# Ending the output projection's first step tile by tile, gating inside PSUM, and moving three groups of copies and sums

## The chip, the cores and the metric

The kernel runs on one core of one Trainium2 chip. The metric is the time of one execution in microseconds (us), as the device measures it; the median of three runs is compared. Beside the timed runs one execution was taken by the hardware profiler, and all rows below come from it. A core has a matrix engine (TensorE, PE in the rows; PEld is its weight load), VectorE (DVE), ScalarE (ACT), GpSimd (POOL) and SyncE (SP), which here only issues DMA transfers. Matrix products land in PSUM, eight banks of 128 x 512 fp32 (the tensor `ps`, indexed by bank); everything else lies in SBUF.

## What is computed

One layer of a diffusion backbone over 1024 tokens of width 1024 (cut to what matters here):

```
y_x = merge(fourier_branch, retention_branch)        # (1024, 1024)
x   = x + g1 * (y_x @ w_out)                         # the "output projection" and its gated residual
h2  = rms_norm(x) * norm2_gain * (1 + sc2) + sh2
x   = x + g2 * (square(relu(h2 @ w_mlp1)) @ w_mlp2)  # MLP, D_FF = 4096
out = rms_norm(x) * final_gain
```

## The kernel before, in words

**Three products for one.** Each fp32 operand is split into a rounded part (`_hi`, made by ACT) and a remainder (`_lo`, made by DVE or POOL), and a product is three matmuls: hi x hi, hi x lo, lo x hi (`mm3`, lines 2159 to 2161). There is no scheduler: each engine has its own instruction list, written out by hand, and waits on semaphores. An engine runs its list strictly in order.

**The output projection** has 16 output tiles (128 tokens x 512 channels), in 4 steps of 4 tiles. Steps 0 and 1 are the two column halves of tokens 0 to 511, steps 2 and 3 those of tokens 512 to 1023. A tile sums over 8 channel tiles `kt`, in 4 weight chunks `kp` of two each (`("wo", n)` in a ring of six slots; ACT rounds a chunk at line 852, POOL makes its remainder at line 772). Step 0 is written apart (`out_first`): for each `kp` it first does the two matmuls with `yT_hi` for all four tiles (lines 2546, 2547: 16 matmuls), and then the one with `yT_lo` for all four (line 2553: 8 matmuls), since the last rows of `yT_lo` come late (line 1790 on DVE, the eighth channel tile). Steps 1 to 3 (`out_step`) use `mm3` and do a chunk's six matmuls of one tile behind each other. Tile i goes to bank `out_bank(i)` and may start when `o_free` is at least i - 3.

**The gated residual** (`residual(step, t)` on DVE) takes a finished tile out: it multiplies the bank by the gate row `g1b` into the SBUF tile `gated` (line 1801) and then adds `gated` to the x rows in `acc` (line 1804). `o_free` counts the multiplications, `x2_done` the additions of a token tile's second half; the stores to `x2_scr` on SP and the squares on ACT (`z_square`) wait for `x2_done`.

**The up projection** (`up(p, j)` on PE, lines 2632 to 2645) works by seven products p = 1 to 7 for each column pair j = 0 to 15, combined with sums of operands and results. A `up` is 12 matmuls. From j = 1 on the order on PE is (1, j+1), (3, j), (2, j+1), (4, j), (6, j+1), (5, j+1), (7, j+1). Products 1, 6, 7 and 4 pile up in one bank; between two of them ACT copies the bank out (`copy_up`, line 1238, into `uw` or `uv`), and the next waits for that copy. DVE adds such a copy to another bank (`add_up`, line 1981) when a quadrant of the result is complete; (3, j) may start when the sum "22" of its pair has been made. Weights of pair j + 2 are loaded, summed (`w_sums`, lines 1891 to 1897), rounded (`w_his`, line 1186) and split (`w_los`, line 1903) meanwhile, unit by unit, in the order of `LATER_UNITS` = B11, B21, T2, T1, T3, B22, T4. `ff_sums` (lines 1993 to 2000) sums results for the down projection.

**The down projection** (`down(s)` on PE, s = 0 to 111) has seven passes q = 0 to 6 of 16 steps n, each of 12 matmuls. Six slots (`LEAD`) hold the operands of coming steps; per step DVE makes two remainders (`s_lo` line 2043, `t_lo` line 2047) and in most passes one sum (line 2035 in pass 2, `b<-t_raw,b`), and PE's step waits for them. Between these, DVE takes finished results out: in passes 2 and 5, `take` (line 2084) and `add_gated` (lines 2079, 2080) add one block of 128 x 512 to the stream `x2`, one block behind each of the steps n = 5, 6, 7 and 8:

```
if q == 2 and 5 <= n < 9:
    dve.wait_ge(down_copied, n - 4)
    take(1, n - 5, BANK_C, p1)
    add_gated(n - 5, 0, (n - 5) % 2)
```

## Time and profile before

| what | us |
|---|---|
| median of 3 runs (lowest, highest) | 1341.75 (1339.44, 1341.82) |
| the profiled execution's own time | 1339.81 |
| its span, first to last instruction | 1338.0 |
| PE busy in the span | 1303.7 |
| DVE / ACT / POOL busy | 806.1 / 559.9 / 185.9 |

The mean granted TensorE clock of the span is 0.996 of full speed (2.4 GHz). A row's "busy" counts an instruction from start to end; matmuls are pipelined, so that the next one starts before the last has ended.

### The profile page before, as it was taken

To read this page: it belongs to the slowest core of one execution; us is meant where nothing else is said; L and a number is where in the kernel's file an instruction comes from. 1 tells how busy PE (TensorE), PEld (TensorE's weight loads), DVE (VectorE), ACT (ScalarE), POOL (GpSimd) and SP (SyncE) were. 2 spreads that over 40 slices of the span, in tenths; PEclk is the share of its full clock that TensorE was granted. 3 is DMA by queue.
4 is the path that set the end of the run, shared out by engine and by line. 5 is a ranking of instruction groups with operands and counts; after the bars stand their busy time and mean duration, and the time that the engine had idled before them with its cause. 6 is when DMAs were issued, how large, how long until landed. Compare 5 with 4: busy or idle time off the path is not lost.

```text
span 1338.0 us, 16538 instructions
## 1 busy us (share of the span) xinstructions
PE 1303.7 (97%) x6236; PEld 1063.6 (79%) x6236; DVE 806.1 (60%) x1270; ACT 559.9 (42%) x939; POOL 185.9 (14%) x103
## 2 busy tenths in 40 slices
PE   4999999999999999999999999999999999999997
PEld 0878788888888788888788878888888887888886
DVE  3563577752663434347568765665564678768866
ACT  5872221241121112114367754555454543545444
POOL 1116330111332222212450000000000000000000
PEclk9899999999999999999999999999999999999999
DMA  9304220201254444438533354444437987568634
GB/s 377 146 32 142 80 95 1 64 28 49 66 176 136 126 127 139 128 112 313 171 128 118 126 173 155 153 163 137 153 124 253 318 278 236 164 190 272 193 105 163
DMA packets 88471, 204.35 MB, mean 153 GB/s; under 512 B 11700, under 2 KB 11956, under 8 KB 87368
## 3 DMA queue, kind: packets, MB, share of 16 engines
q1 hardware_dynamic: 75552, 170.18, 38.0%
q10 hardware_dynamic: 11048, 26.82, 6.3%
q0 software_dynamic: 1792, 6.29, 1.4%
q8 instruction: 50, 0.82, 0.3%
q14 instruction: 29, 0.24, 0.1%
HBM read 159.72 MB, written 43.53 MB: 152 GB/s over the span
## 4 chain that ended last, share of the span: by engine, by line
PE 90%; DVE 4%; DMA 4%; ACT 1%; issue 1%; SPq 1%; ACTq 0%; DVEq 0%
PE ps L2159 19%; PE ps L2161 19%; PE ps L2160 19%; PE ps L2632 7%; PE ps L2640 7%; PE ps L2635 7%; PE ps L2658 3%; DMA raw<-in_w_stream 2%; PE ps L2230 2%; PE ps L2351 1%; PE ps L2197 1%; DMA ada_raw<-in_w_ada 1%; PE ps L2205 1%; PE ps L2333 1%; PE ps L2292 1%
## 5 line engine op out<-in xcount | busy, mean ns | idle before, releaser
L772 POOL TENSOR_TENSOR ring_lo<-raw,ring_hi 128x1024 fp32r<-128x1024 f32 x58 | 140.7, 2433 | 484.0 <-ACT ring_hi L852 483.9
L2159 PE MATMUL ps<-t_hi,s_hi 128*128 128x512 f32 x392 | 153.2, 391 | 1.2 <-DVE t_lo L2047 1.2
L2161 PE MATMUL ps<-t_hi,s_lo 128*128 128x512 f32 x392 | 153.1, 391 | 0.0
L2160 PE MATMUL ps<-t_lo,s_hi 128*128 128x512 f32 x392 | 153.1, 391 | 0.0
L2159 PE MATMUL ps<-hT_hi,ring_hi 128*128 128x512 f32 x320 | 125.0, 391 | 0.0
L2161 PE MATMUL ps<-hT_hi,ring_lo 128*128 128x512 f32 x320 | 124.5, 389 | 0.0
L2160 PE MATMUL ps<-hT_lo,ring_hi 128*128 128x512 f32 x320 | 124.5, 389 | 0.0
L1268 ACT ACTIVATE s_hi<-s_raw 128x512 fp32r<-128x512 f32 x112 | 70.6, 630 | 117.1 <-DMA b<-in_w_stream 57.5
L852 ACT ACTIVATE ring_hi<-raw 128x1024 fp32r<-128x1024 f32 x62 | 64.9, 1057 | 110.7 <-PE ps L2161 53.8
L2043 DVE TENSOR_TENSOR s_lo<-s_raw,s_hi 128x512 fp32r<-128x512 f32 x112 | 77.3, 690 | 47.9 <-ACT s_hi L1268 47.4
L1754 DVE SCALAR_TENSOR_TENSOR ada_acc<-ada_raw,silu_c,ada_acc 128x1024 f32<-128x1024 f32 x28 | 44.4, 1584 | 98.6 <-DMA ada_raw<-in_w_ada 98.4
L2159 PE MATMUL ps<-ring_hi,hT_hi 128*128 128x512 f32 x232 | 94.1, 406 | 0.0
L2161 PE MATMUL ps<-ring_hi,hT_lo 128*128 128x512 f32 x232 | 90.6, 391 | 0.0
L2160 PE MATMUL ps<-ring_lo,hT_hi 128*128 128x512 f32 x232 | 90.5, 390 | 0.0
L2159 PEld LDWEIGHTS ps<-t_hi,s_hi 128*128 128x128 f32 x392 | 73.6, 188 | 17.6 <-DVE t_lo L2047 1.8
L2161 PEld LDWEIGHTS ps<-t_hi,s_lo 128*128 128x128 f32 x392 | 73.6, 188 | 15.8
L2160 PEld LDWEIGHTS ps<-t_lo,s_hi 128*128 128x128 f32 x392 | 73.6, 188 | 15.8
L2159 PEld LDWEIGHTS ps<-hT_hi,ring_hi 128*128 128x128 f32 x320 | 60.1, 188 | 14.9 <-issue 2.6
L2161 PEld LDWEIGHTS ps<-hT_hi,ring_lo 128*128 128x128 f32 x320 | 60.1, 188 | 12.6
L2160 PEld LDWEIGHTS ps<-hT_lo,ring_hi 128*128 128x128 f32 x320 | 60.1, 188 | 12.3
L1256 ACT ACTIVATE ffa<-ffa 128x512 f32<-128x512 f32 x48 | 30.3, 631 | 73.6 <-DVE ffa L1981 73.6
L2159 PEld LDWEIGHTS ps<-ring_hi,hT_hi 128*128 128x128 f32 x232 | 43.6, 188 | 10.6 <-issue 1.5
(404 smaller groups left out, 2807.9 us busy)
## 6 DMA issues: line engine op xcount, KB each, us to landing
s_raw<-ff_scr SPq DMA_DIRECT2D x112, 256.0 KB, 2.9
raw<-in_w_stream SPq DMA_DIRECT2D x50, 512.0 KB, 3.6
ada_raw<-in_w_ada ACTq DMA_DIRECT2D x32, 512.0 KB, 4.3
ff_scr<-ffs SPq DMA_DIRECT2D x16, 1024.0 KB, 5.1
t_raw<-in_w_stream SPq DMA_DIRECT2D x64, 256.0 KB, 3.4
w_B_raw<-in_w_stream SPq DMA_DIRECT2D x48, 256.0 KB, 2.8
ff_scr<-ffa SPq DMA_DIRECT2D x16, 768.0 KB, 4.5
b<-in_w_stream SPq DMA_DIRECT2D x48, 256.0 KB, 4.5
```

The source lines that it names most:

```text
L772: nc.gpsimd.tensor_tensor(lo_ap, raw_of(i), hi_ap.bitcast(F32), ALU.subtract).then_inc(split, 1)
L852: A(slot(c)[0], raw_of(i), ACT.Copy).then_inc(hi_done, 1)
L1268: A(s_slot[n][0][:], s_slot[n][2][:], ACT.Copy).then_inc(down_hi, 1)
L1754: do.chain(V.scalar_tensor_tensor(ada_acc[:], ada_raw[:], silu_c[:, kt, 0:1], ada_acc[:], ALU.mult, ALU.add), ada_acc_done)
L2043: V.tensor_tensor(s_slot[n][1][:], s_slot[n][2][:], s_slot[n][0][:].bitcast(F32), ALU.subtract).then_inc(down_lo, 1)
L2159: M(dst, lhsT=l_hi, rhs=r_hi, start=first, stop=False, skip_group_check=goes_on)
L2160: M(dst, lhsT=l_hi, rhs=r_lo, start=False, stop=False, skip_group_check=goes_on)
L2161: return M(dst, lhsT=l_lo, rhs=r_hi, start=False, stop=last, skip_group_check=goes_on)
L2632: M(ps[:, b, :], lhsT=l_hi[:, w], rhs=m_hi[:, kt, :], start=kt == 0 and not adds, stop=False, skip_group_check=adds)
L2635: M(ps[:, b, :], lhsT=l_hi[:, w], rhs=m_lo[:, kt, :], start=False, stop=False, skip_group_check=adds)
L2640: mm = M(ps[:, b, :], lhsT=l_lo[:, w], rhs=m_hi[:, kt, :], start=False, stop=kt == 3 and (p, j) != (6, 0), skip_group_check=adds)
L2658: mm = M(ps[:, down_bank(q, sub), :], lhsT=left[:, sub * P:(sub + 1) * P], rhs=right[:], start=False, stop=False)
```

## The change

It has four parts.

1. Step 0 of the output projection keeps `out_first` for `kp` = 0 to 2; its last chunk (`kp` = 3, channel tiles 6 and 7) is done by a new function `out_first_end`, tile by tile: six matmuls for a tile, then the next tile. The matmuls are the same 24, in another order.
2. `residual` writes the gated product back to its PSUM bank and adds from there; `gated` goes. `o_free` now counts the additions, and takes over what `x2_done` did (`row_added`).
3. In the up projection the pair behind j = 2 is ordered like that behind j = 1: ACT's `copy_up(6, 3)` stands ahead of the rounding of T2 and T1, `copy_up(7, 3)` ahead of T3, B22 and T4, and DVE's sum "22" of pair 3 ahead of the remainders of T3, B22 and T4.
4. In passes 2 and 5 of the down projection the four blocks for `x2` stand behind steps n = 5, 7, 9 and 11.

```
@@ -281,7 +281,6 @@
         hq = place("hq", o_t, [P, KT, 2 * P])
         g1b = place("g1b", o_t + 8192, [P, D])
         b1b = place("b1b", o_t + 14336, [P, D])
-        gated = place("gated", o_t + 12288, [P, 512])
 
         junk3 = place("junk3", o_t + 8192, [P, D])
 
@@ -392,7 +391,6 @@
         g_ready = sem("g_ready")
         o_done = sem("o_done")
         o_free = sem("o_free")
-        x2_done = sem("x2_done")
         a_hi = sem("a_hi")
         a11_lo = sem("a11_lo")
         a12_lo = sem("a12_lo")
@@ -532,6 +530,10 @@
 
             return i - 2 if i in (2, 3) else 4 + i % 4
 
+        def row_added(eng, t):
+
+            eng.wait_ge(o_free, t + (5 if t < 4 else 9))
+
         def main_wait(eng, i):
 
             if i >= 2:
@@ -589,7 +591,7 @@
         @block.sync
         def _(sp):
             def store_x2(t):
-                sp.wait_ge(x2_done, t + 1)
+                row_added(sp, t)
                 sp.dma_start(x2_scr[t], acc[:, t % 4, :]).then_inc(x2_stored[t % 4], 16)
 
             sp.dma_start(dist[:], ins["dist"]).then_inc(decay_in, 16)
@@ -1113,7 +1115,7 @@
             hi_to(("wo", 12))
 
             def z_square(t):
-                act.wait_ge(x2_done, t + 1)
+                row_added(act, t)
                 act.wait_ge(sumsq, 10 + t)
                 if t == 0:
                     act.wait_ge(gates_done, 2 * KT)
@@ -1317,18 +1319,20 @@
                     w_his(j + 2, LATER_UNITS[:2])
                 if j > 1:
                     relu_square("21", j)
+                if j == 2:
+                    copy_up(6, j + 1)
                 if j + 2 < FP:
                     w_his(j + 2, LATER_UNITS[2:4])
-                if j == 1:
+                if j in (1, 2):
                     copy_up(7, j + 1)
-                if j > 1 and not last:
+                if j > 2 and not last:
                     copy_up(6, j + 1)
                 if j == FP - 2:
                     down_his(0)
                 if j + 2 < FP:
                     w_his(j + 2, LATER_UNITS[4:])
                 if not last:
-                    if j > 1:
+                    if j > 2:
                         copy_up(7, j + 1)
                     relu_square("22", j + 1)
 
@@ -1798,10 +1802,10 @@
                 if nh == 0:
                     dve.wait_ge(acc_in[t % 4], 16 * (t // 4 + 1))
                 dve.wait_ge(o_done, i + 1)
-                do.chain(V.tensor_tensor(gated[:], ps[:, out_bank(i), :], g1b[:, nh * 512:(nh + 1) * 512], ALU.mult),
-                         o_free)
+                gated = ps[:, out_bank(i), :]
+                do.chain(V.tensor_tensor(gated, gated, g1b[:, nh * 512:(nh + 1) * 512], ALU.mult))
                 dst = acc[:, t % 4, nh * 512:(nh + 1) * 512]
-                do.chain(V.tensor_tensor(dst, dst, gated[:], ALU.add), x2_done if nh else None)
+                do.chain(V.tensor_tensor(dst, gated, dst, ALU.add), o_free, i + 1)
 
             def z_mean(first, last):
                 n = max(first - 3, 0) + 1
@@ -2065,11 +2069,14 @@
                 if j == 1:
                     add_up("22", j + 1)
                 ff_sums(j)
+                if j == 2:
+                    w_los(j + 2, LATER_UNITS[2:4])
+                    add_up("22", j + 1)
                 if j + 2 < FP:
-                    w_los(j + 2, LATER_UNITS[2:])
+                    w_los(j + 2, LATER_UNITS[4 if j == 2 else 2:])
                 if j == FP - 2:
                     down_los(0)
-                if j > 1 and not last:
+                if j > 2 and not last:
                     add_up("22", j + 1)
 
             def add_gated(t, nh, first, signal=None):
@@ -2116,10 +2123,11 @@
                     dve.wait_ge(x2_in, 16 * 2)
                 if s == 5 * FP + 4:
                     dve.wait_ge(x2_in, 16 * 4)
-                if q == 2 and 5 <= n < 9:
-                    dve.wait_ge(down_copied, n - 4)
-                    take(1, n - 5, BANK_C, p1)
-                    add_gated(n - 5, 0, (n - 5) % 2)
+                if q == 2 and n in (5, 7, 9, 11):
+                    t = (n - 5) // 2
+                    dve.wait_ge(down_copied, t + 1)
+                    take(1, t, BANK_C, p1)
+                    add_gated(t, 0, t % 2)
                 if q == 3 and 6 <= n < 10:
                     t = n - 6
                     dve.wait_ge(down_copied, 4 + t + 1)
@@ -2127,10 +2135,11 @@
                     do.chain(V.tensor_tensor(x2[:, t, 512:], x2[:, t, 512:], out_u[:, t % 2, :], ALU.add), x2_sum)
                 if q == 3 and 10 <= n < 14:
                     early_gain(n - 10)
-                if q == 5 and 5 <= n < 9:
-                    dve.wait_ge(down_copied, 8 + n - 4)
-                    take(4, n - 5, BANK_B, pw)
-                    add_gated(4 + n - 5, 1, (n - 5) % 2)
+                if q == 5 and n in (5, 7, 9, 11):
+                    t = (n - 5) // 2
+                    dve.wait_ge(down_copied, 8 + t + 1)
+                    take(4, t, BANK_B, pw)
+                    add_gated(4 + t, 1, t % 2)
                 if q == 5 and 9 <= n < 13:
                     early_gain(4 + n - 9)
                 if q == 5 and n == 14:
@@ -2540,7 +2549,7 @@
                     for e in range(2):
                         kt = 2 * kp + e
                         if t == 0:
-                            pe.wait_ge(*((y_hi_done, kt + 1) if kt < KT - 1 else (y_split, KT)))
+                            pe.wait_ge(y_hi_done, kt + 1)
                         cs = slice(e * 512, (e + 1) * 512)
                         toks = slice(t * P, (t + 1) * P)
                         M(ps[:, out_bank(t), :], lhsT=yT_hi[:, kt, toks], rhs=r_hi[:, cs], start=kt == 0, stop=False)
@@ -2549,19 +2558,30 @@
                     for e in range(2):
                         kt = 2 * kp + e
                         if t == 0:
+                            pe.wait_ge(y_split, kt + 1)
+                        mm = M(ps[:, out_bank(t), :], lhsT=yT_lo[:, kt, t * P:(t + 1) * P],
+                               rhs=r_hi[:, e * 512:(e + 1) * 512], start=False, stop=False)
+                mm.then_inc(used, 1)
+
+            def out_first_end():
+
+                r_hi, r_lo = chunk(("wo", 3))
+                for t in range(4):
+                    toks = slice(t * P, (t + 1) * P)
+                    for kt in (KT - 2, KT - 1):
+                        if t == 0:
                             pe.wait_ge(y_split, kt + 1 + (kt == KT - 1))
-                        mm = M(ps[:, out_bank(t), :], lhsT=yT_lo[:, kt, t * P:(t + 1) * P],
-                               rhs=r_hi[:, e * 512:(e + 1) * 512], start=False, stop=kt == KT - 1)
-                    if kp == 3:
-                        mm.then_inc(o_done, 1)
-                    elif t == 3:
-                        mm.then_inc(used, 1)
-
-            for kp in range(4):
+                        cs = slice(kt % 2 * 512, (kt % 2 + 1) * 512)
+                        mm = mm3(ps[:, out_bank(t), :], yT_hi[:, kt, toks], yT_lo[:, kt, toks], r_hi[:, cs], r_lo[:, cs],
+                                 False, kt == KT - 1)
+                    mm.then_inc(o_done, 1)
+
+            for kp in range(3):
                 out_first(kp)
                 if kp == 1:
                     pe.wait_ge(gates_done, 2 * KT)
                     reduce_row(3, 2)
+            out_first_end()
             for step in range(1, 3):
                 for kp in range(4):
                     for t in range(4):
```

How the first part moves instructions on PE, at the last chunk of step 0. Before, the last rows of the chunk: pairs of matmuls with the rounded `yT_hi` (two for each channel tile of a token tile), and then all eight with `yT_lo`, ahead of step 1, which begins with line 2159.

```order
L2546 MATMUL ps<-ring_hi,yT_hi 128x512
L2547 MATMUL ps<-ring_lo,yT_hi 128x512
L2546 MATMUL ps<-ring_hi,yT_hi 128x512
L2547 MATMUL ps<-ring_lo,yT_hi 128x512
L2553 MATMUL ps<-ring_hi,yT_lo 128x512 x8
L2159 MATMUL ps<-ring_hi,yT_hi 128x512
```

Now, from the end of the third chunk on (line 2562 is its eight matmuls with `yT_lo`); lines 2168 to 2170 are `mm3`, and two such threes are one tile.

```order
L2556 MATMUL ps<-ring_lo,yT_hi 128x512
L2562 MATMUL ps<-ring_hi,yT_lo 128x512 x8
L2168 MATMUL ps<-ring_hi,yT_hi 128x512
L2169 MATMUL ps<-ring_lo,yT_hi 128x512
L2170 MATMUL ps<-ring_hi,yT_lo 128x512
L2168 MATMUL ps<-ring_hi,yT_hi 128x512
L2169 MATMUL ps<-ring_lo,yT_hi 128x512
L2170 MATMUL ps<-ring_hi,yT_lo 128x512
```

The matmuls with `yT_lo` have moved from the end of the chunk to each tile's place, so a tile is complete after every sixth matmul of the chunk.

How the third part moves ACT's instructions, after the sum "12" and "11" of its turn j = 2. Line 1238 (1240 now) is `copy_up`, with `uv` for product 6 and `uw` for product 7; line 1186 (1188 now) rounds a unit of the weights. Before:

```order
L1250 ACTIVATE a_229<-ps 128x512
L1252 ACTIVATE a_229<-a_229 128x512
L1186 ACTIVATE w_T_hi<-w_T_raw 128x512 x2
L1238 ACTIVATE uv_231<-ps 128x512
L1186 ACTIVATE w_T_hi<-w_T_raw 128x512
L1186 ACTIVATE w_B_hi<-w_B_raw 128x512
L1186 ACTIVATE w_T_hi<-w_T_raw 128x512
L1238 ACTIVATE uw<-ps 128x512
```

Now:

```order
L1252 ACTIVATE a_228<-ps 128x512
L1254 ACTIVATE a_228<-a_228 128x512
L1240 ACTIVATE uv_230<-ps 128x512
L1188 ACTIVATE w_T_hi<-w_T_raw 128x512 x2
L1240 ACTIVATE uw<-ps 128x512
L1188 ACTIVATE w_T_hi<-w_T_raw 128x512
L1188 ACTIVATE w_B_hi<-w_B_raw 128x512
L1188 ACTIVATE w_T_hi<-w_T_raw 128x512
```

Both copies have moved up by one group of roundings.

And on DVE, in the same turn, from `ff_sums` on (line 1903, now 1907, makes a remainder; line 1981, now 1985, is `add_up`). Before:

```order
L2000 TENSOR_TENSOR ffs_227<-ffa_225,ffs_227 128x512
L1903 TENSOR_TENSOR w_T_lo<-w_T_raw,w_T_hi 128x512 x3
L1903 TENSOR_TENSOR w_B_lo<-w_B_raw,w_B_hi 128x512
L1903 TENSOR_TENSOR w_T_lo<-w_T_raw,w_T_hi 128x512
L1981 TENSOR_TENSOR ffa_226<-ps,uw 128x512
```

Now:

```order
L2004 TENSOR_TENSOR ffs_226<-ffa_224,ffs_226 128x512
L1907 TENSOR_TENSOR w_T_lo<-w_T_raw,w_T_hi 128x512 x2
L1985 TENSOR_TENSOR ffa_225<-ps,uw 128x512
L1907 TENSOR_TENSOR w_T_lo<-w_T_raw,w_T_hi 128x512
L1907 TENSOR_TENSOR w_B_lo<-w_B_raw,w_B_hi 128x512
L1907 TENSOR_TENSOR w_T_lo<-w_T_raw,w_T_hi 128x512
```

The sum stood behind five remainders and stands behind two.

## Rows read from the trace of the kernel before

**Rows 1.** The page's first part: engine, busy us (share of the span), instructions.

```profile
PE 1303.7 (97%) x6236; PEld 1063.6 (79%) x6236; DVE 806.1 (60%) x1270; ACT 559.9 (42%) x939; POOL 185.9 (14%) x103
```

**Rows 2.** PE's waits: line, releaser: us in total, times, longest.

```profile
PE ps L2256 <- DMA ada_in<-in_w_ada: 14.4, 8, 8.8
PE ps L2197 <- issue: 4.7, 1, 4.7
PE ps L2159 <- DVE gated L1801: 2.2, 2, 1.6
PE ps L2159 <- DVE t_lo L2047: 1.2, 1, 1.2
PE ps L2632 <- ACT uv L1238: 1.1, 1, 1.1
...
PE ps L2632 <- DVE ffa L1981: 0.7, 1, 0.7
```

**Rows 3.** Timeline of PE, projection: start, us, instruction, [idle before it <- releaser].

```profile
632.33 0.39 PE L2546 MATMUL ps<-ring_hi,yT_hi 128*128 128x512 f32 x1
...
635.96 1.98 PE L2553 MATMUL ps<-ring_hi,yT_lo 128*128 128x512 f32 x8
...
639.93 0.47 PE L2159 MATMUL ps<-ring_hi,yT_hi 128*128 128x512 f32 x1 [0.64 <-DVE gated L1801]
...
644.61 0.47 PE L2159 MATMUL ps<-ring_hi,yT_hi 128*128 128x512 f32 x1 [1.61 <-DVE gated L1801]
```

**Rows 4.** Timeline of DVE around the same place.

```profile
629.66 1.23 DVE L1790 TENSOR_TENSOR yT_lo<-y,yT_hi 128x1024 fp32r<-128x1024 f32 x1
...
636.71 0.69 DVE L1801 TENSOR_TENSOR gated<-ps,g1b 128x512 f32<-128x512 f32 x1 [4.56 <-PE ps L2553]
637.43 1.62 DVE L1804 TENSOR_TENSOR acc<-acc,gated 128x512 f32<-128x512 f32 x1
...
641.27 2.48 DVE L1804 TENSOR_TENSOR acc<-acc,gated 128x512 f32<-128x512 f32 x1
643.78 0.69 DVE L1801 TENSOR_TENSOR gated<-ps,g1b 128x512 f32<-128x512 f32 x1
```

**Rows 5.** Timeline of POOL there.

```profile
633.75 4.76 POOL L772 TENSOR_TENSOR ring_lo<-raw,ring_hi 128x1024 fp32r<-128x1024 f32 x2 [4.67 <-ACT ring_hi L852]
640.80 2.40 POOL L772 TENSOR_TENSOR ring_lo<-raw,ring_hi 128x1024 fp32r<-128x1024 f32 x1 [2.29 <-ACT ring_hi L852]
```

**Rows 6.** Line 1504 (rotary step): count: ns min/median/max, first and last start.

```profile
L1504 DVE TENSOR_TENSOR ps<-ps,rope x16: 699/700/700, 58.0 to 240.4; 128x512 f32<-128x512 f32 x16
```

**Rows 7.** Tile `acc`, the last of its four loads: issue and landing.

```profile
L1097 ACTq DMA_DIRECT2D acc<-in_x x1: 484/484/484, 623.0 to 623.0; - x1
...
DMA to landing us min/median/max: 8.7/8.7/8.7
```

**Rows 8.** Timeline of PE, up projection: first matmuls of (7, 3) and (3, 3).

```profile
783.57 0.47 PE L2632 MATMUL ps<-h_hi,w_T_hi 128*128 128x512 f32 x1 [1.09 <-ACT uv L1238]
...
789.98 0.47 PE L2632 MATMUL ps<-s_hi,w_B_hi 128*128 128x512 f32 x1 [0.72 <-DVE ffa L1981]
```

**Rows 9.** Timeline of ACT there.

```profile
782.85 0.58 ACT L1238 ACTIVATE uv<-ps 128x512 f32<-128x512 f32 x1
```

**Rows 10.** Timeline of DVE there.

```profile
779.74 0.69 DVE L1891 TENSOR_TENSOR w_T_raw<-w_B_raw,w_T_raw 128x512 f32<-128x512 f32 x1 [4.75 <-DMA w_B_raw<-in_w_stream]
...
786.14 1.89 DVE L1903 TENSOR_TENSOR w_T_lo<-w_T_raw,w_T_hi 128x512 fp32r<-128x512 f32 x3
...
789.15 0.68 DVE L1981 TENSOR_TENSOR ffa<-ps,uw 128x512 f32<-128x512 f32 x1
```

**Rows 11.** Timeline of DVE, pass 2 of the down projection: starts of steps 5, 9, 10.

```profile
1116.81 0.69 DVE L2035 TENSOR_TENSOR b<-t_raw,b 128x512 f32<-128x512 f32 x1
...
1133.49 0.69 DVE L2035 TENSOR_TENSOR b<-t_raw,b 128x512 f32<-128x512 f32 x1
...
1135.49 0.68 DVE L2035 TENSOR_TENSOR b<-t_raw,b 128x512 f32<-128x512 f32 x1
```

**Rows 12.** Timeline of PE, first matmul of step 9 of that pass.

```profile
1135.63 0.50 PE L2159 MATMUL ps<-t_hi,s_hi 128*128 128x512 f32 x1 [1.15 <-DVE t_lo L2047]
```

More of the change, by code:

```diff
@@ L283, in program @@
         b1b = place("b1b", o_t + 14336, [P, D])
-        gated = place("gated", o_t + 12288, [P, 512])
         junk3 = place("junk3", o_t + 8192, [P, D])
@@ L533, in out_bank, with row_added @@
             return i - 2 if i in (2, 3) else 4 + i % 4
+        def row_added(eng, t):
+            eng.wait_ge(o_free, t + (5 if t < 4 else 9))
         def main_wait(eng, i):
@@ L1319, in _ @@
                     relu_square("21", j)
+                if j == 2:
+                    copy_up(6, j + 1)
                 if j + 2 < FP:
                     w_his(j + 2, LATER_UNITS[2:4])
-                if j == 1:
+                if j in (1, 2):
                     copy_up(7, j + 1)
-                if j > 1 and not last:
+                if j > 2 and not last:
                     copy_up(6, j + 1)
@@ L2067, in _ @@
                 ff_sums(j)
+                if j == 2:
+                    w_los(j + 2, LATER_UNITS[2:4])
+                    add_up("22", j + 1)
                 if j + 2 < FP:
-                    w_los(j + 2, LATER_UNITS[2:])
+                    w_los(j + 2, LATER_UNITS[4 if j == 2 else 2:])
                 if j == FP - 2:
                     down_los(0)
-                if j > 1 and not last:
+                if j > 2 and not last:
                     add_up("22", j + 1)
@@ L2118, in _ @@
                     dve.wait_ge(x2_in, 16 * 4)
-                if q == 2 and 5 <= n < 9:
-                    dve.wait_ge(down_copied, n - 4)
-                    take(1, n - 5, BANK_C, p1)
-                    add_gated(n - 5, 0, (n - 5) % 2)
+                if q == 2 and n in (5, 7, 9, 11):
+                    t = (n - 5) // 2
+                    dve.wait_ge(down_copied, t + 1)
+                    take(1, t, BANK_C, p1)
+                    add_gated(t, 0, t % 2)
                 if q == 3 and 6 <= n < 10:
@@ L2129, in _ @@
                     early_gain(n - 10)
-                if q == 5 and 5 <= n < 9:
-                    dve.wait_ge(down_copied, 8 + n - 4)
-                    take(4, n - 5, BANK_B, pw)
-                    add_gated(4 + n - 5, 1, (n - 5) % 2)
+                if q == 5 and n in (5, 7, 9, 11):
+                    t = (n - 5) // 2
+                    dve.wait_ge(down_copied, 8 + t + 1)
+                    take(4, t, BANK_B, pw)
+                    add_gated(4 + t, 1, t % 2)
                 if q == 5 and 9 <= n < 13:
```

38 lines of the change are left out of this document (23 added, 15 removed).

## The prediction, made before the changed kernel had run

> **What bounds the kernel now.** I read the page's table of engines first: PE is busy for 1303.7 of 1338.0 us [rows 1], so no other engine's work can shorten the kernel, only PE's own waits can. Then PE's waits [rows 2]. The two longest stand in the start-up (lines 2256 and 2197), which the change does not touch. Behind the start-up five waits matter, together 5.2 us: two on `gated` (2.2), one on `t_lo` (1.2), one on `uv` (1.1), one on `ffa` (0.7). The change touches the making of all four. Then the timeline at each.
>
> A wait costs more than its idle time. Eight matmuls take 1.98 us and one 0.39 [rows 3], so they start (1.98 - 0.39) / 7 = 0.227 us apart; after a wait the engine idles from the end of the last one, which adds 0.39 - 0.23 = 0.16, and the first matmul lasts 0.47 or 0.50 instead of 0.39, which delays the next by 0.08 or 0.11. So each wait costs its idle time plus 0.24 (0.27).
>
> **Part 1 and 2, the projection.** Before: 0.64 + 0.24 and 1.61 + 0.24 = **2.73 us** [rows 3]. The reason is in [rows 4]: all four tiles of step 0 end within the last eight matmuls, DVE gets the first at 636.71, and then needs 0.72 for a multiplication (636.71 to 637.43) and 0.7 for an addition, if undisturbed. But the additions at 637.43 and 641.27 last 1.62 and 2.48, and end 0.54 and 0.55 us after POOL's instructions beside them (633.75 + 4.76 = 638.51; 640.80 + 2.40 = 643.20) [rows 5]. The multiplication at 636.71, with one input in PSUM, lasts 0.69 inside POOL's span.
>
> After, tile by tile. The chunk starts at 632.33; the last matmul of tile k (0 to 3) starts (6k + 5) x 0.227 later: 633.47, 634.83, 636.19, 637.55. DVE began 0.52 after such a start before (the first tile's second matmul with `yT_lo` started at 635.96 + 0.23 = 636.19, DVE at 636.71). So the tiles are there at 633.98, 635.35, 636.71 and 638.07. A residual is a multiplication from PSUM into PSUM, for which line 1504 shows the form, 0.70 us [rows 6], and an addition with one input in PSUM, taken as 0.69 like the multiplication of the kernel before; with the hand-overs of 0.03 seen there 1.45 in all. The additions end at 635.43, 636.88, 638.33 and 639.78. PE restarted 0.14 after the releasing instruction (643.78 + 0.69, 644.61), and would want the four banks at 637.78 + 0.227 x 6k: 637.78, 639.14, 640.50, 641.86. The spare time is 2.2, 2.1, 2.0 and 1.9 us: both waits go, and the later release (behind the addition, +0.73) costs nothing while this cover stands. Without it, each bank would come 0.73 later.
>
> What could spoil it. The eighth channel tile's remainder is now wanted at the fourth matmul, 632.33 + 3 x 0.227 = 633.01, where it was wanted at 636.19; it ends at 629.66 + 1.23 = 630.89 [rows 4]: 2.1 spare. The x rows: the last load was issued at 623.0 and landed 8.7 later, 631.7 [rows 7], ahead of 633.98. Bounds for what has no row of its own (an addition out of PSUM right behind a write into it): from 0.69 up to 1.2, as if half again were added; at 1.2 a residual takes 1.96 and the fourth ends at 633.98 + 7.84 = 641.82, 0.1 us late for PE. **Gain 2.73, at least 2.6.**
>
> The Trainium skill ("SBUF — State Buffer", section "Who interferes with whom") says that a VectorE instruction with two SBUF inputs contends with a GpSimd instruction that reads SBUF, and that one with at most one SBUF input does not. Both halves agree with the rows above. By it the new additions are never caught; without it, see the second rival.
>
> **Part 3, the up projection.** Before: 1.09 + 0.24 and 0.72 + 0.24 = **2.29 us** [rows 8]. The first: (7, 3) waits for ACT's copy into `uv` at 782.85 [rows 9], which stands behind two roundings, and these behind DVE's weight sums, which begin at 779.74 when a load has landed after 4.75 us of idling [rows 10]. Now the copy stands ahead of them. It needs only (6, 3), which ends 12 matmuls (2.72 us) ahead of (5, 3)'s end, so it is done long before (7, 3) comes up. That wait goes: (7, 3) starts at 783.57 - 1.09 - 0.16 = 782.32. (1, 4) follows, and (3, 3) comes up 24 matmuls later, at 787.77.
>
> The second: (3, 3) waits for the sum "22", at 789.15 [rows 10], and restarted at 789.98, 0.83 after its start. DVE's queue up to there is still tied to the load at 779.74; three remainders in a row take 1.89, so one frees the queue after 0.60 ((1.89 - 0.69) / 2). The sum now stands behind two remainders: 786.14 + 1.20 = 787.34. Its other input, `uw`, needs (7, 3) done (782.32 + 11 x 0.227 + 0.39 = 785.2) and one copy of 0.6: 785.9, earlier. So (3, 3) starts at 787.34 + 0.83 = 788.17: a wait of 0.40 stays, with 0.08 behind it. **Gain 2.29 - 0.48 = 1.81.** Bounds: 1.33, if the second wait stays whole, and 2.29. Behind the moved copies ACT's three other roundings and DVE's three remainders are about 1 us later; they serve products of pair 4 that PE reaches over 10 us later, since a turn of seven products takes 19 us.
>
> **Part 4, the down projection.** Before: 1.15 + 0.27 = **1.42 us** [rows 12]. Step 5 of pass 2 begins on DVE at 1116.81 and step 9 at 1133.49: 4.17 us a step with a block for `x2`, 2.00 without (to 1135.49) [rows 11], against 2.72 on PE. So DVE falls back by 1.45 a step four times over, and the remainder of step 9 ends just ahead of PE's restart at 1135.63, that is 2.08 after the step's start. PE wanted it 1.31 earlier, at 1134.32.
> With the blocks at 5, 7, 9 and 11 step 12 starts at 1116.81 + 4 x 4.17 + 3 x 2.00 = 1139.49 and its remainder ends at 1141.57; PE wants it at 1134.32 + 3 x 2.72 = 1142.48. That is the narrowest place: 0.9 spare (step 10: 1.6). The wait goes. DVE is never waiting for loads there, so its own pace decides. **Gain 1.42**, bounds 0.5 (if 0.9 more than the spare time is lost) and 1.42. Pass 5 has no wait of PE [rows 2], and its blocks come later but long before pass 6 needs their bank.
>
> **The sum.** 2.73 + 1.81 + 1.42 = 5.96 us. Everything behind the projection is set off by PE or by loads that PE's progress releases, so the time should reach the end. The profiled execution took 1339.81 (span 1338.0): 1333.85 and 1332.0. That execution lies 1.9 below the median of 1341.75, near the fastest of the three (1339.44); set against the median the forecast is 1341.75 - 6.0 = **1335.7**. The smallest difference that can be told from none is about 0.2%, 2.7 us.
>
> **The rivals.**
> 1. *One wait comes back.* DVE at step 12 has 0.9 to spare and the sum "22" is tied to a load. If the down wait returns and the second up wait stays whole, 5.96 - 1.42 - 0.48 = 4.1 is left: 1337.7. For it: both chains hang on DVE's pace. Against it: both are worked out from one trace in which they fit. Still faster than the bound.
> 2. *The additions are caught by POOL although one input is in PSUM.* Then the addition at 634.71 ends at 639.05 as that of 637.43 did, tile 1's at 640.50, and tile 2's at 643.75 like the one at 641.27. PE is held at 640.64 (1.5 late) and at 643.89, 3.4 late in all, and up to 2.2 more if a third is caught. Against 2.73 before that is a loss of 0.7 to 2.9; with the other gains (3.23) the kernel takes 1339.2 to 1341.4. Against it: the multiplication at 636.71.
> 3. *The time does not reach the end*, because a load or a later wait grows by as much (say at the load that ended 4.75 us of idling on DVE): around 1341, no difference. Against it: between the named places PE shows no wait of note, and the loads are released by PE.
> 4. *The other side: the release behind the addition.* A bank is now held for both operations, four in a row 5.8 us. If the first residual starts at T, the fourth bank is there for PE at T + 5.94, against 644.61 before. With T = 633.98 this is hidden; from T = 638.7, 4.7 us later, this stage is slower than before, and to end 2.7 us slower in all T must lie at 644.6 (3.23 more for the other gains). What can shift T is the last remainder: it stands behind two instructions that POOL holds back, and one more such delay is at most a POOL instruction, 2.4 us; that would cost PE 0.3. It would take several: 1344.5 or more.
>
> **How the numbers follow.** All three stages as worked out: 0.73. Rival 1: 0.15. Rival 2: 0.04. Rival 3: 0.05. Rival 4: 0.03. The terms' bounds give gains of 2.6 + 1.33 + 0.5 = 4.4 to 6.44, so 1335.3 to 1337.3; the median of three lies anywhere in a spread of 2.4 us (1339.44 to 1341.82), mostly downwards from the middle. Range 1333.2 to 1338.2, which takes in rival 1. Faster: 0.73 + 0.15 = 0.88; same: rivals 2 and 3, 0.09; slower: 0.03.
>
> **What would show it.** PE's waits: no entry for the residual's lines or for `uv`; `t_lo` gone; at the sum "22" a wait of about 0.2 idle. The residual's additions all at 0.7, also inside POOL's spans. DVE's first residual at 634.0. Wrong would be: additions of 1.6 to 2.5 us, a wait at 633 for line 1794's `yT_lo`, or a `t_lo` wait at step 12.

## The result, and the profile after

| | before | after |
|---|---|---|
| median us (lowest to highest), 5 runs each, side by side | 1339.44 (1338.0 to 1341.82) | 1332.25 (1330.96 to 1332.83) |
| span of the profiled execution | 1338.0 | 1330.4 |

The ratio is 0.9947, 95% interval 0.9935 to 0.9959: faster by 7.2 us, with 5.5 to 8.7 by the interval. The five runs of before include the three whose median was 1341.75. The direction and all three places are as forecast. The time is 3.4 us below the 1335.7 forecast and 0.95 below the range.

PE's busy time has not changed (1304.2 against 1303.7 in [rows 1]); what has gone is waiting. The waits of PE after (line, releaser: us in total, times, longest), to be held against [rows 2]:

```profile
PE ps L2265 <- DMA ada_in<-in_w_ada: 13.6, 7, 8.5
PE ps L2206 <- issue: 2.7, 1, 2.7
PE ps L2239 <- ACT kT L859: 1.0, 4, 0.3
PE ps L2273 <- DVE mod_rows L1482: 0.8, 1, 0.8
PE ps L2239 <- ACT xh_b L1136: 0.2, 1, 0.2
```

No entry is left for the residual, `uv`, `ffa` or `t_lo`; only the start-up and small waits on transposes remain. The timeline of DVE in the projection (start, us, instruction, idle before it), against [rows 4]; lines 1806 and 1808 are the multiplication and the addition:

```profile
628.50 1.22 DVE L1794 TENSOR_TENSOR yT_lo<-y,yT_hi 128x1024 fp32r<-128x1024 f32 x1
...
632.83 0.70 DVE L1806 TENSOR_TENSOR ps<-ps,g1b 128x512 f32<-128x512 f32 x1 [1.85 <-PE ps L2170]
633.56 0.69 DVE L1808 TENSOR_TENSOR acc<-ps,acc 128x512 f32<-128x512 f32 x1
634.28 0.70 DVE L1806 TENSOR_TENSOR ps<-ps,g1b 128x512 f32<-128x512 f32 x1
...
637.93 0.69 DVE L1808 TENSOR_TENSOR acc<-ps,acc 128x512 f32<-128x512 f32 x1
```

and that of POOL and PE beside it:

```profile
632.89 4.87 POOL L774 TENSOR_TENSOR ring_lo<-raw,ring_hi 128x1024 fp32r<-128x1024 f32 x2 [4.97 <-ACT ring_hi L854]
```

```profile
631.17 0.39 PE L2168 MATMUL ps<-ring_hi,yT_hi 128*128 128x512 f32 x1
...
636.61 0.39 PE L2168 MATMUL ps<-ring_hi,yT_hi 128*128 128x512 f32 x1
```

The last chunk begins 1.16 earlier in this execution than in the trace of before (631.17, 632.33 in [rows 3]), so the first residual was due at 633.98 - 1.16 = 632.82, and began at 632.83. The additions last 0.69 inside POOL's span, where additions with two inputs in SBUF lasted 1.62 and 2.48 [rows 4]; a residual takes 1.45 (634.28 - 632.83). Step 1 follows the 24 matmuls without a gap (636.61 - 631.17 = 24 x 0.227).

The up projection, DVE (against [rows 10]) and PE:

```profile
781.96 1.29 DVE L1907 TENSOR_TENSOR w_T_lo<-w_T_raw,w_T_hi 128x512 fp32r<-128x512 f32 x2
783.16 0.68 DVE L1985 TENSOR_TENSOR ffa<-ps,uw 128x512 f32<-128x512 f32 x1
```

```profile
783.99 0.47 PE L2652 MATMUL ps<-s_hi,w_B_hi 128*128 128x512 f32 x1
```

The sum "22" stands 1.20 behind the start of the remainders, as forecast, and (3, 3) starts 0.83 behind it. Its start comes 0.51 after that of the matmul before, so a delay of 0.28 is left, with 0.08 behind it (0.40 and 0.08 forecast). In the down projection's pass 2 the steps with a block take 4.17 and those without 2.00, as forecast, and PE does not wait at step 12, which begins on DVE at the last of these rows:

```profile
1111.46 0.69 DVE L2039 TENSOR_TENSOR b<-t_raw,b 128x512 f32<-128x512 f32 x1
1115.62 0.69 DVE L2039 TENSOR_TENSOR b<-t_raw,b 128x512 f32<-128x512 f32 x1
1117.62 0.69 DVE L2039 TENSOR_TENSOR b<-t_raw,b 128x512 f32<-128x512 f32 x1
...
1134.12 0.69 DVE L2039 TENSOR_TENSOR b<-t_raw,b 128x512 f32<-128x512 f32 x1
```

The remainder that PE needs for this step was ready barely in time: in down_only, where PE did wait for it, PE restarted 2.14 behind the start of DVE's step 12 (1139.63 to 1141.77), which here gives 1134.12 + 2.14 = 1136.26, and PE begins its step 12 at

```profile
1136.38 0.40 PE L2168 MATMUL ps<-t_hi,s_hi 128*128 128x512 f32 x1
```

That leaves 0.12 us to spare in this execution, where 0.9 was forecast.

The mechanisms are there one for one. The question that the experiments had to answer is where the other 1.2 us of gain come from, and the 2.3 by which the median of the first three runs of before (1341.75) lay above that of all five (1339.44).

**How stretches are measured.** Between the first matmul of the projection with `yT_hi`, the first of the up projection and the first of the down projection PE's work is the same in every kernel here, so the distances between these matmuls in PE's timeline, and that to PE's last, show what each stage loses. In a trace of after they are 93.63, 303.23 and 312.30, in the trace of before 96.51, 305.16 and 313.88: 2.88 + 1.93 + 1.58 = 6.39 us. The 1.16 by which the projection began earlier stands ahead of them all and belongs to the start-up, which the change does not touch.

### The profile page after: what moved, and what is told of

Its sections match the earlier page's. It is cut to its first block, busy times and chain, and to the rows that moved or that the text cites. A ratio compares the mean times of both kernels' runs of the same rounds, so it can differ in the third digit from the quotient of the medians.

```text
span 1330.4 us, 16538 instructions
## 1 busy us (share of the span) xinstructions
PE 1304.2 (98%) x6236; PEld 1064.5 (80%) x6236; DVE 801.0 (60%) x1270; ACT 560.4 (42%) x939; POOL 185.9 (14%) x103
## 4 chain that ended last, share of the span: by engine, by line
PE 95%; DMA 2%; DVE 1%; ACT 1%; SPq 0%; issue 0%; ACTq 0%; DVEq 0%
PE ps L2168 20%; PE ps L2170 20%; PE ps L2169 20%; PE ps L2652 7%; PE ps L2660 7%; PE ps L2655 7%; PE ps L2678 3%; DMA raw<-in_w_stream 2%; PE ps L2239 2%; PE ps L2360 1%; PE ps L2206 1%; PE ps L2214 1%; PE ps L2342 1%; PE ps L2301 1%; PE ps L2208 1%; PE ps L2352 1%
```

## The experiments

The theory when they began: the terms are right in kind, and the size is off by what one execution shows. The rivals: another part of the kernel gains too; or the parts are worth something else than was argued. Ratios are to runs of the kernel before on the same chip, with 95% intervals; the columns "stretches" are the three above.

| kernel | median us | ratio | stretches |
|---|---|---|---|
| before_again | 1338.88 | 1.0001 (0.9992 to 1.001) | 97.38, 304.96, 314.46 |
| before_third | 1341.18 (one run) | | 97.79, 305.01, 314.27 |
| before_fourth | 1336.41 (one run) | | 95.16, 305.09, 314.13 |
| tile_end (part 1) | 1335.93 | 0.9973 (0.9962 to 0.9984) | 93.78, 305.01, 314.30 |
| psum_only (part 2) | 1336.79 | 0.998 (0.9971 to 0.9989) | 94.55, 305.14, 313.49 |
| tile_end_psum (1 and 2) | 1335.49 | 0.9971 (0.996 to 0.9981) | 93.63, 304.97, 314.59 |
| up_only (part 3) | 1337.57 | 0.9983 (0.9974 to 0.9992) | 97.36, 303.25, 315.00 |
| down_only (part 4) | 1337.6 | 0.9985 (0.9976 to 0.9994) | 97.03, 304.96, 312.73 |
| three_parts (without part 2) | 1331.66 | 0.9944 (0.993 to 0.9958) | 93.69, 303.27, 312.30 |
| after_again | 1331.48 | 0.9942 (0.9929 to 0.9954) | 93.63, 303.27, 312.30 |
| two_more | 1331.36 | 0.9938 (0.9925 to 0.995) | 93.63, 302.71, 312.30 |
| gates_early | 1336.83 | 0.9978 (0.9968 to 0.9989) | 97.31, 305.09, 312.30 |

**The kernel before, and the changed one, once more.** No edit.

> The kernel before, unchanged, profiled once more. Two theories on the 1.2 us by which the changed kernel's trace is ahead already at the first matmul on yT_hi (613.66 against 614.82 us), a place that the change does not touch. Chance of the start-up (loads of ada_in, the first weights): this trace lies anywhere between some 613 and 616 at that place, and before the first ring_hi,hc_hi matmul it waits for a time other than the 4.7 us seen. Layout of the program: it comes at 614.8 again. Both: ratio 1.000 within its interval; behind that place the trace repeats 96.5 us to the first up product, 305.2 to the first down step and 313.9 to PE's end, within 0.3.

> The changed kernel once more. If its gain is the sum of the three stages, 6.4 us, and the rest chance: ratio 0.9952, within 0.9942 to 0.9962, and the place of the first yT_hi matmul somewhere else than 613.66. If the 7.2 us seen are the change's own: 0.9947 again and that place at 613.7 again.

The expectation that before_again would repeat 96.5, 305.2 and 313.9 within 0.3 failed in two of three stretches (97.38 and 314.46). Stretches in which PE has no wait repeat within 0.01 us (93.63 in four traces, 312.30 in five; only three_parts has 93.69). The start of the projection, 614.82 in the trace of the prediction and 613.66 in that of after, came at 612.59 in before_again and 612.71 in after_again, and lies between 612.59 and 614.82 in all fourteen traces, so the 1.16 between the first two is chance of the start-up and not a difference of the programs. The ratio of after_again, 0.9942, lies on the edge of the 0.9942 to 0.9962 expected for a gain of 6.4 us. The waits of PE in before_again:

```profile
PE ps L2159 <- DVE gated L1801: 3.2, 2, 1.9
...
PE ps L2159 <- DVE t_lo L2047: 1.5, 2, 1.2
```

These were 2.2 and 1.2 in [rows 2], with one wait on `t_lo`, not two.

**Part 1 alone.** The last chunk tile by tile, `gated` in SBUF as before:

```
-            for kp in range(4):
+            for kp in range(3):
                 out_first(kp)
...
+            out_first_end()
```

> Only the new order of the last chunk of step 0; the gated product goes through SBUF and the bank is free behind the multiplication, as before. My theory (POOL holds back the additions with two SBUF inputs): the first residual starts 2.7 us earlier, but its addition waits for POOL's pair of instructions, and the third addition for the next one, so that PE waits about 0.8 and 2.0 us: nearly the 2.7 of before; ratio 1.000, change 0 to -0.6 us. Rival (the spacing of the tiles is what counts, POOL or not): both waits go, -2.7 us, ratio 0.998.

My theory fell, and the rival held: part 1 alone takes nearly the whole loss out of the stretch (93.78, where 93.63 is left without any wait). The timeline of DVE shows why:

```profile
632.77 0.69 DVE L1801 TENSOR_TENSOR gated<-ps,g1b 128x512 f32<-128x512 f32 x1 [1.99 <-PE ps L2161]
...
634.95 2.05 DVE L1804 TENSOR_TENSOR acc<-acc,gated 128x512 f32<-128x512 f32 x1
637.03 0.69 DVE L1801 TENSOR_TENSOR gated<-ps,g1b 128x512 f32<-128x512 f32 x1
637.76 2.05 DVE L1804 TENSOR_TENSOR acc<-acc,gated 128x512 f32<-128x512 f32 x1
639.85 0.69 DVE L1801 TENSOR_TENSOR gated<-ps,g1b 128x512 f32<-128x512 f32 x1
```

```profile
640.68 0.47 PE L2159 MATMUL ps<-ring_hi,yT_hi 128*128 128x512 f32 x1
```

Two additions are still held, and last 2.05 us. But DVE starts on the first tile 3.8 us ahead of PE's step 1 (636.55), where it was 1.1 in before (636.71, with the 24 matmuls from 632.33 over at 637.78), and here a bank is released by the multiplication. The last bank is free at 639.85 + 0.69 = 640.54, and PE, which wants it at 640.64 (24 + 18 matmuls after the chunk's start at 631.11), starts at 640.68: no idle time, but nothing to spare either.

**Part 2 alone, and with part 1.**

```
-                do.chain(V.tensor_tensor(gated[:], ps[:, out_bank(i), :], g1b[:, nh * 512:(nh + 1) * 512], ALU.mult),
-                         o_free)
+                gated = ps[:, out_bank(i), :]
+                do.chain(V.tensor_tensor(gated, gated, g1b[:, nh * 512:(nh + 1) * 512], ALU.mult))
...
-                do.chain(V.tensor_tensor(dst, dst, gated[:], ALU.add), x2_done if nh else None)
+                do.chain(V.tensor_tensor(dst, gated, dst, ALU.add), o_free, i + 1)
```

> Only the gated product in PSUM, with the release behind the addition; the order of the last chunk as before. My theory: additions all 0.7, releases at 1.45 us steps from the first tile at 636.7, so PE waits about 0.5 once and 0.1 three times: 0.8 in place of 2.8, change -2.0 us, ratio 0.9985. Rival (the later release costs): the bank comes 0.7 later each time, PE waits 2.7 or more, no gain.

> Both parts in the projection, nothing else. My theory: no wait of PE between the first projection matmul and the first up product; -2.8 us, ratio 0.9979; the stretch from the first yT_hi matmul to the first up product 93.6 us as in the whole change. If the whole change's 7.2 us were more than the sum of its parts, this would show less than -2.5.

Alone, part 2 makes all additions 0.69, and 0.92 us of loss is left (94.55 against 93.63, 0.8 expected), so the rival of a later release that costs the whole gain is out. It leaves one wait of PE, on the first addition, since the bank now comes behind both operations and the tiles still end together:

```profile
636.13 0.47 PE L2161 MATMUL ps<-ring_hi,yT_hi 128*128 128x512 f32 x1 [0.35 <-DVE acc L1806]
```

Together they give the 93.63 that was expected, without a wait of PE. The two parts do not add: 3.2 us and 2.4 us alone, 3.3 together, all against 96.93, the mean of the stretch over the seven traces in which both places are as before the change.

**The change without part 2.** As this says that part 2 is worth 0.15 at most, it was tried: the changed kernel with `residual`, `o_free` and `x2_done` as before.

> The changed kernel without its part 2 (the gated product is again put into an SBUF tile, and a bank is released behind the multiplication). My theory from the runs so far: once the tiles end six matmuls apart (part 1), the additions are still held until a POOL instruction ends (two of them at 2.05 us in the run of part 1 alone), but the spacing and the release behind the multiplication absorb it, so part 2 is worth only the 0.15 us by which the stretch from the first matmul of the projection to the first of the up projection was longer there (93.78 against 93.63). Expected: that stretch 93.7 to 93.9, PE without a wait on `gated` over 0.1 us, the time within 0.3 us of the changed kernel's, ratio to before 0.9945. The rival (the prediction's reading: both parts are needed, since DVE is held by POOL): a wait on `gated` of 1 us or more comes back, stretch 95 or more, ratio 0.9955 or higher.

The theory held: 93.69, no wait on `gated`, a ratio that can't be told from that of the whole change. Three additions are held and last 1.87, 2.05 and 2.30 us, and PE does not wait for them:

```profile
632.86 1.87 DVE L1806 TENSOR_TENSOR acc<-acc,gated 128x512 f32<-128x512 f32 x1
...
635.49 2.05 DVE L1806 TENSOR_TENSOR acc<-acc,gated 128x512 f32<-128x512 f32 x1
...
639.75 2.30 DVE L1806 TENSOR_TENSOR acc<-acc,gated 128x512 f32<-128x512 f32 x1
```

**Parts 3 and 4 alone.**

```
+                if j == 2:
+                    w_los(j + 2, LATER_UNITS[2:4])
+                    add_up("22", j + 1)
```

```
-                if q == 2 and 5 <= n < 9:
+                if q == 2 and n in (5, 7, 9, 11):
```

> Only the earlier copies and sum in the up projection. My theory: the wait for uv goes, of the wait for the sum 22 some 0.3 to 0.5 stays; the stretch from the first up product to the first down step falls from 305.2 to 303.3 us, change -1.9 us, ratio 0.9986. Rival (the gain needs the shift of the projection): the wait comes back with the load it hangs on, under 1 us.

> Only the blocks for x2 in every second step. My theory: the t_lo wait goes, the stretch from the first down step to PE's end falls from 313.9 to 312.3 us, change -1.5 us, ratio 0.9989, and step 12's remainder ends 0.9 us ahead of PE. Rival (DVE's total is what counts): the wait moves to a later step and the gain is under 0.7.

Part 3 takes the up stretch from 305.04 (mean of the nine traces with the old order) to 303.25: 1.8 us, in every trace alike. The gain does not need the shift of the projection, so the rival is out, and the wait that is left is 0.2, not 0.3 to 0.5. Part 4 brings the down stretch to 312.73, where 312.3 was expected: most of the gain, so DVE's total is not what counts, but one short wait is left, at step 12, in this execution:

```profile
1141.77 0.50 PE L2161 MATMUL ps<-t_hi,s_hi 128*128 128x512 f32 x1 [0.18 <-DVE t_lo L2047]
```

Step 5 began on DVE 101.40 after the first matmul of the down projection here, and 100.32 in the trace of the prediction (1116.81 - 1016.49), for which 0.9 to spare was worked out. A start 1.08 later should then have been about 0.2 too late. PE was in fact 0.34 late (0.18 of idle time and the 0.16 by which the idle time is shorter than the delay), so the trace of the prediction had 0.7 to spare and not 0.9. That place is indeed the narrowest.

**A step more in the same direction.** In the changed kernel the sum "22" of pair 3 stands ahead of all five remainders; and `residual(3, 7)` stands ahead of `s2_sum(0)`.

```
                 if j == 2:
-                    w_los(j + 2, LATER_UNITS[2:4])
                     add_up("22", j + 1)
...
-            s2_sum(0)
             residual(3, 7)
+            s2_sum(0)
```

> The changed kernel with the sum 22 of pair 3 ahead of all five remainders, and the last residual of the projection (3, 7) ahead of s2_sum(0). My theory: the wait of 0.28 + 0.08 at (3, 3) and the one of 0.41 at the transposes of xh behind the second up product both go: -0.8 us against the changed kernel, ratio to before 0.9946 if that has 0.9952. Rival: s2_sum, 1.45 later, holds back s1_sum and the weight sums of pair 1, and a wait appears at the first up products that takes it back.

The up stretch loses another 0.52 to 0.56 (0.8 expected), and `ffa` and `xh_b` are gone from the waits, with no new wait in their place, so the rival is out; in the total (1331.36 against 1331.48 in after_again) that can't be told from nothing.

**Two more executions of the kernel before.** No edit.

> The kernel before, unchanged, once more. Theory on the size of the miss: the waits that the change removes differ from one execution to the next, and the one trace of the prediction had short ones. Over the runs that kept the old order they cost 2.8 to 3.7 us in the projection and 1.1 to 2.7 us in pass 2 of the down projection. Expected here: projection 93.63 plus 2.8 to 3.7 = 96.4 to 97.4, from the first down projection matmul to PE's end 312.30 plus 1.1 to 2.7 = 313.4 to 315.0, and in pass 2 a cost that rises with the start of DVE's step 5 relative to PE's. Rival (the waits are steady, and the miss is a difference of executions outside these stretches): 96.5 and 313.9 again, each within 0.1.

> The same kernel a fourth time, with the same expectations: projection 96.4 to 97.4 and down projection 313.4 to 315.0 by the theory of waits that vary, 96.5 and 313.9 by the rival. The sum over both stretches, averaged over the traces of the kernel before, should come out 0.9 to 1.4 us above that of the trace of the prediction.

The down stretches lie within what was expected (314.27 and 314.13). The waits in the projection vary more than I said: 97.79 and 95.16, where 96.4 to 97.4 was expected, and so the mean over the four traces of the kernel before lies only 0.5 above the first one (sum of projection and down stretches: 410.39, 411.84, 412.06, 409.29), not 0.9 to 1.4. The rival of steady waits is out. What makes them vary: an addition that is held ends 0.55 after POOL's instruction, so its length is set by where in POOL's instruction it begins. In before_fourth, of the first four additions only the second and the fourth were caught, and one of the two waits was absent:

```profile
635.21 0.69 DVE L1804 TENSOR_TENSOR acc<-acc,gated 128x512 f32<-128x512 f32 x1
...
636.66 2.05 DVE L1804 TENSOR_TENSOR acc<-acc,gated 128x512 f32<-128x512 f32 x1
...
639.47 0.69 DVE L1804 TENSOR_TENSOR acc<-acc,gated 128x512 f32<-128x512 f32 x1
```

In before_third two were caught early in POOL's instructions and lasted 2.83 and 2.54 us, and the stretch is the longest.

**What sets the wait in the down projection.** Over the eight traces that keep the old order of both blocks and loads, what PE loses in pass 2 (the starts of its matmuls that come more than 0.227 apart) goes with the start of DVE's step 5, counted from the first matmul of the down projection:

| | psum_only | before | fourth | third | tile_end | again | tile_end_psum | up_only |
|---|---|---|---|---|---|---|---|---|
| step 5 starts | 99.90 | 100.32 | 100.58 | 100.68 | 100.76 | 100.87 | 101.05 | 101.45 |
| PE loses | 1.13 | 1.50 | 1.75 | 1.88 | 1.92 | 2.08 | 2.23 | 2.65 |

The difference is 98.77 to 98.84 everywhere. From step 2 to step 5 DVE does not wait (7.24 us), and step 2 waits for a load; in before:

```profile
1109.57 0.69 DVE L2035 TENSOR_TENSOR b<-t_raw,b 128x512 f32<-128x512 f32 x1 [4.26 <-DMA t_raw<-in_w_stream]
```

SP issues it right behind three loads that are wanted only at step 4:

```profile
1099.67 0.43 SPq L733 DMA_DIRECT2D g2b<-mod_scr  x1
1100.14 0.43 SPq L734 DMA_DIRECT2D b2b<-in_b_ada  x1
1100.62 0.43 SPq L735 DMA_DIRECT2D fgb<-in_final_gain  x1
...
1101.91 0.59 SPq L714 DMA_DIRECT2D t_raw<-in_w_stream  x1
```

So they were issued 23 steps earlier, in the kernel before, with nothing else changed:

```
-                if s == 2 * FP + 1:
+                if s == FP - 6:
                     sp.wait_ge(row_stored, 16 * 8)
                     sp.dma_start(g2b[:], mod_scr[3:4, :].to_broadcast([P, D])).then_inc(gates_in, 16)
```

> The kernel before, with the three broadcast loads of `g2b`, `b2b` and `fgb` issued 23 steps earlier (behind step 10 of pass 0, not behind step 1 of pass 2). In the traces so far the load of `t_raw` for step 2 of pass 2 stands right behind them in SP's queue and lands 7.6 us after its issue, where 3.7 is the median; DVE waits for it, and the cost in pass 2 is the start of step 5, counted from the first matmul of the down projection, less 98.81. Theory (these loads make step 2's load late, and so set the wait): step 2 starts on DVE at or before 91.5 instead of 92.6 to 94.2, step 5 at 98.8 or earlier, PE has no wait on `t_lo` in pass 2, and the stretch from the first matmul of the down projection to PE's end is 312.3 to 312.6, with the time at about 1337.3 by this alone. Rival (the load is late because all DMA engines are busy with the weights of pass 1, whatever stands ahead of it): step 2 still starts at 92.6 or later, with 1.1 to 2.7 us of waits and a stretch of 313.4 to 315.0.

The theory held. The load for step 2, issued 85.4 us after the first matmul of the down projection in both kernels, landed 3.0 us after its issue and not 7.6 (7.2 to 8.8 in the thirteen traces with the old order of loads). Step 2 starts at 88.48, step 5 at 97.04 (98.8 is where waiting begins), and PE has no wait on `t_lo`, with the blocks still at 5, 6, 7 and 8. The rows of DVE's steps 2 and 3:

```profile
1104.98 0.68 DVE L2035 TENSOR_TENSOR b<-t_raw,b 128x512 f32<-128x512 f32 x1
1107.64 0.69 DVE L2035 TENSOR_TENSOR b<-t_raw,b 128x512 f32<-128x512 f32 x1 [0.59 <-DMA t_raw<-in_w_stream]
```

The stretch is 312.30, as in the changed kernel, and the ratio 0.9978 (1.5 to 4.3 us) agrees with a loss of about 2 us. This edit together with part 4 was not run.

## Why the prediction was right, and where it was wrong

**The time that the gain was taken from: wrong, and the main error.** The step that failed is "set against the median the forecast is 1341.75 - 6.0 = 1335.7". The profiled execution had taken 1339.81, and 1341.75 was the middle of three runs, a small sample: sets of 5 to 25 runs of the same kernel give medians of 1338.59 to 1339.44. The same gain of 6.0 taken from the profiled execution gives 1333.85, and from 1339.44 it gives 1333.5, 1.2 us above the measured time. The text had both figures and chose the one that did not go with the terms: all terms were read from the execution of 1339.81. Of the 3.4 us by which the forecast missed, 2.3 lie here (1341.75 - 1339.44), and the rest in the size of the gain. It took both to leave the range of 1333.2 to 1338.2: with the gain right and only this time wrong the kernel would have taken 1339.44 - 5.96 = 1333.5, and with this time right and only the gain wrong 1341.75 - 7.2 = 1334.55.

**The size of the gain: 5.96 forecast, 7.2 measured, too small by 1.2.** 5.96 lies in the interval of the ratio, 5.5 to 8.7, but the traces show where the rest is. The means of the traces with the old order are 96.93 for the projection (seven traces), 305.04 for up (nine) and 314.27 for down (eight); less 93.63, 303.25 and 312.30:

| term | forecast | same pair of traces | mean of the traces |
|---|---|---|---|
| projection | 2.73 | 2.88 | 3.30 |
| up | 1.81 | 1.93 | 1.79 |
| down | 1.42 | 1.58 | 1.97 |
| sum | 5.96 | 6.39 | 7.06 |

The mis-sized terms are thus the first and the third: "0.64 + 0.24 and 1.61 + 0.24" and "1.15 + 0.27" were one execution's waits. Over the traces these waits cost between 1.5 and 4.2 us in the projection and between 1.1 and 2.7 in the down projection. Within the one pair of traces 0.43 more went than was added up: 0.12 because less of the second up wait stayed (0.36, not 0.48), the rest mostly in delays of under 0.1 us each on PE that the text did not count. The range took the spread of the medians into account and not that of the waits: its bound of 6.44 was the largest gain that the one trace allowed.

**Parts 1 and 2: the mechanisms right, their roles wrong.** The first residual started within 0.01 us of its forecast time, a residual took the 1.45 that was worked out, and no addition with an input in PSUM was held. That "both waits go" holds; but the prediction left open which part does it, and its "the reason is in [rows 4]" puts the held additions beside the tiles that end together. three_parts shows that the spacing alone is enough: the holds are there and cost nothing. Part 2 only gives the spare time back that the holds take: at the fourth bank tile_end has nothing left (it starts 0.04 late), where after has the 1.9 that was worked out (the fourth addition ends at 638.62, and 0.14 later is 638.76; PE wants the bank at 640.70). Rival 2's price (0.7 to 2.9 us worse) rested on holds together with the release behind the addition, a pair that no kernel here has.

**Part 3: right.** The first wait goes, of the second 0.28 + 0.08 is left (0.40 + 0.08), and no run brought it back.

**Part 4: right in kind, and narrower than said.** "0.9 spare" at step 12 was 0.7, as down_only shows, and 0.12 in the trace of after, whose step 5 started later (100.94 against 100.32). It is a reserve against the load of step 2, and step 5 started up to 1.13 later in other executions (101.45): the four traces with parts 1, 3 and 4 (after, after_again, three_parts and two_more, 100.27 to 100.94) show no wait, and down_only, at 101.40, does. That pass 2 lost nothing there is thus partly luck, and by the latest start seen, 101.45, the changed kernel could lose an estimated 0.5 us there in some executions. The prediction said that DVE "is never waiting for loads there, so its own pace decides". From step 2 on that is so; but where its pace begins is set by the load at step 2, with 4.26 us of idling just ahead of the rows that it had read, and the same load, delayed by three others, is why before waited there at all (gates_early).

**Rivals.** 1 happened in a small form once (down_only, 0.43 us). 2 did not: no addition with an input in PSUM was caught. 3 and 4 did not: what PE saved reached the end whole. From the end of PE's last matmul to that of the span it is 7.6 us in every trace.

## What to carry to other kernels

A wait read from one trace is one draw: where what ends it is a load's landing, or the place of one engine's instruction within another's, profile the same kernel two or three times and take the mean before pricing its removal, and take the gain from the time of the execution that the terms were read from. For a wait of an engine that runs at its own pace, follow the chain back to where it last stood still; taking three loads out of the way of the one that it had stood still for removed the wait as well as a change to the pace did. When tiles that are taken out by another engine all end together, try spacing their ends first: here that alone gave 3.2 us, and with it in place the shorter additions gave less than 0.2 more.

## What the runs showed of the hardware

**A slower clock that cost nothing.** In before_third PE stood still for 1.84 us, and half a microsecond later its matmuls started 0.39 and then, seven times, 0.43 apart instead of 0.227. PE's rows, and the same core in windows (the third number from the end, 0.50 and 1.00, is the granted clock):

```profile
640.99 0.47 PE L2159 MATMUL ps<-ring_hi,yT_hi 128*128 128x512 f32 x1 [1.84 <-DVE gated L1801]
...
641.92 0.63 PE L2159 MATMUL ps<-ring_hi,yT_hi 128*128 128x512 f32 x1
642.35 0.63 PE L2160 MATMUL ps<-ring_lo,yT_hi 128*128 128x512 f32 x1
...
645.74 0.47 PE L2159 MATMUL ps<-ring_hi,yT_hi 128*128 128x512 f32 x1 [0.18 <-DVE gated L1801]
```

```profile
641.60:644.80 3.20, 3.20 (x9) 2.52 (x8) 3.16 (x2) 2.40 (x4) 2.37 (x1) 0.50 0.27 109
...
645.00:650.00 5.00, 4.82 (x22) 3.67 (x21) 3.26 (x5) 1.06 (x1) 3.12 (x2) 1.00 0.66 204
```

The clock was at 0.50, the 1.2 GHz level, throughout the first window, and PE's matmuls came 0.16 + 7 x 0.20 = 1.6 us later by it. But the next bank was what PE had to wait for in any case. It was freed by the multiplication behind the second held addition, on DVE:

```profile
642.33 2.54 DVE L1804 TENSOR_TENSOR acc<-acc,gated 128x512 f32<-128x512 f32 x1
644.90 0.69 DVE L1801 TENSOR_TENSOR gated<-ps,g1b 128x512 f32<-128x512 f32 x1
```

These work on tiles of step 0, which PE had finished before the slow stretch, and 644.90 + 0.69 + 0.15 is PE's 645.74. At the full clock PE would have stood there for about 1.8 us and not 0.18. So the slow matmuls took the place of idle time, and the stretch of 97.79 is that of two long holds. In before_again a wait of 1.93 us was followed by no such drop, so what decides it stays open, and no run shows a wait whose removal also saved a loss of clock.

**Held additions.** An addition with two inputs in SBUF that began inside one of POOL's instructions ended 0.54 to 0.56 after that instruction, in all nine traces with such additions (in before_third 642.33 + 2.54 = 644.87 against 641.95 + 2.37 = 644.32), but for one that began in its last 0.1 us and lasted 0.69. One that began before POOL's instruction was not held: in tile_end the addition at 633.50 lasts 0.69, with POOL's instruction beginning at 633.94. None of the 16 additions of each trace with an input in PSUM was held, though five of those in after began inside one of POOL's instructions. The Trainium skill ("SBUF — State Buffer", section "Who interferes with whom") says that a VectorE instruction with two SBUF inputs contends with a GpSimd instruction that reads SBUF, and that one with at most one SBUF input, outside the modes that use two ports, does not. POOL's instructions here read `raw` and `ring_hi`, both in SBUF, and the traces agree with both halves. Multiplying a bank in place took 0.70, and into SBUF 0.69.

**Three loads in the wrong place.** `t_raw` for one step landed 7.2 to 8.8 us after its issue with three broadcast loads just ahead of it in the queue (7.6 in before), and 3.0 us with these loads elsewhere (gates_early).
